# Two transformer blocks on one core: padding the rows of three x buffers in SBUF

## The chip, the cores and the metric

The kernel runs on one core of a Trainium2 chip. The metric is the time of one execution on the device in microseconds (us); lower is better. One execution was also recorded by the profiler, and every row shown here comes from that recording. Engines are called PE (matrix multiply), PEld (its weight load, which overlaps PE), DVE (vector), ACT (scalar), POOL (GpSimd) and SP (which issues most transfers).

## The reference

The input x has 256 rows of 1024 float32 numbers. A first block applies a gated MLP mixer with a spatial 128 x 128 mix, a SwiGLU feed-forward, attention with a relative bias over chunks of 64, a second SwiGLU feed-forward and a norm. A second block runs two layers, each with a mixer (a 31-tap convolution branch, a causal attention branch and a gated linear attention branch, joined and projected) and a feed-forward with a 3-tap convolution, and ends in a norm. Nearly all the arithmetic is in the products `h @ w`, where `h = rms_norm(x, g)` or an activation:

```
h = _rms_norm(x, g_norm);  z = h @ w_in          # gated MLP
gate, up = split(h @ w_gate_up);  y = silu(gate) * up;  x = x + y @ w_down
u = causal_depthwise_conv(h @ ffn_w_up, ...);    x = x + (silu(u0) * u1) @ ffn_w_down
```

## The kernel before

**Weights.** All weights come as a stream of units of 128 partitions x 2048 float32, in four slots (`raw`). For each unit ACT writes a rounded copy `whi` (line 602) and DVE the remainder `wlo` (line 1160), both in the format fp32r. A product of two float32 matrices is then three products in fp32r: high by high, high by low, low by high (`split3`, lines 1875 to 1877). Each matmul has its own weight load.

**x, transposed.** PE turns x (line 1903), DVE multiplies the columns by the norm's gain (`xg`, line 1211), ACT writes the high part `xth` (line 616) and DVE the low part `xtl` (line 1223). Both are tiles of 8 rows (`kt`, one for each 128 of the 1024 model columns) of 256 numbers (the tokens) in every partition. These are the unscaled x: the factor 1/rms of each token is applied later, when a product is read out. An instruction of line 616 or 1223 writes 4 rows, 128 numbers of each.

**Where x is read.** PE reads the tiles in three ways.
- In `in_group` (lines 1875 to 1877) 128 numbers of a row of `xth` or `xtl` are the stationary operand, and 512 columns of `whi` or `wlo` stream past it. The 11th weight part of the mixers does the same with 272 columns of the tiles `whx` and `wlx`, whose rows are 272 numbers (1088 bytes) long and not padded.
- In `kq_step` (lines 2183 to 2186) and in the first feed-forward groups of the second block (`up_straight` for j = 1 and 2, lines 2554 to 2557) the weights are stationary and a whole row of 256 numbers of `xth` or `xtl` streams.
- In `up_straight` for j from 3 to 10 (lines 2545 and 2549) a third tile, `xhl`, streams. Its 8 rows hold the scaled x: 256 high numbers and then 256 low numbers. ACT writes the high halves (line 1086) and DVE the low halves (line 1787), in two instructions each per layer. Line 2545 streams all 512 numbers of a row past `whi`, line 2549 the first 256 past `wlo`.

**Addresses.** Every tile is placed by hand. Offsets such as `o_xh` (of `xth`), `o_xl` (of `xtl`), `o_yh` and `o_yl` (activations), `o_sc` (scratch, `xhl` at `o_sc + 5120`) and `o_c` (constants) are sums of the sizes ahead of them, in float32 numbers from byte 16512 of each partition. The order of work is a fixed list on each engine, held together by semaphores.

Of the kernel before, what the change touches and what calls it, by code (L numbers as in the profile page):

```python
# [21 lines left out]
F32R = mybir.dt.float32r  # L22
# [6 lines left out]
SEQ = 256  # L29
M = SEQ // P  # L30
KT = D // P
# [24 lines left out]
FSEVEN_POS = (6, 8)  # L56


U_IN = 0
U_OUTA = U_IN + 16  # L60
U_GLU0 = U_OUTA + 8
# [23 lines left out]
def two_blocks_kernel(nc, x_in, stream, cols, bs_col, ws_t, gs_row, fin_row, fin2_row, rel_rows, ffn_cw,  # L85
                      conv_w, conv_ln, moba_g, gla_g, gate_w, gate_b, gate_in, out):
    ctx = ExitStack()
    with ctx:
# [5 lines left out]
        def at(name, shape, offset, dt=F32):  # L94
            return nc.alloc_sbuf_tensor_at(name, [P] + shape, dt, offset=base + 4 * offset)
# [2 lines left out]
        o_raw, o_hi, o_lo = 0, SLOTS * UNIT, 2 * SLOTS * UNIT  # L98
        o_x = 3 * SLOTS * UNIT
        o_xh = o_x + M * D  # L100
        o_xl = o_xh + KT * SEQ
        o_yh = o_xl + KT * SEQ
        o_yl = o_yh + 22 * SEQ
        o_sc = o_yl + 22 * SEQ
        o_c = o_sc + 9216
        o_sa, o_sb = o_yh + KT * SEQ, o_yl + KT * SEQ

        raw = at("raw", [SLOTS, UNIT], o_raw)
        whi = at("whi", [SLOTS, UNIT], o_hi, F32R)
        wlo = at("wlo", [SLOTS, UNIT], o_lo, F32R)  # L110
        x = at("x", [M, D], o_x)
        xth = at("xth", [KT, SEQ], o_xh, F32R)
        xtl = at("xtl", [KT, SEQ], o_xl, F32R)
        yth = at("yth", [22 * SEQ], o_yh, F32R)
        ytl = at("ytl", [22 * SEQ], o_yl, F32R)
        yth3 = yth[:, :].rearrange("p (k t) -> p k t", t=SEQ)
# [47 lines left out]
        us = at("us", [2, M, 512], o_sc)  # L164
        cv = at("cv", [2, 4, SEQ], o_sc + 2048)
        pr = at("pr", [2, 2, SEQ], o_sc + 4096)
        xhl = at("xhl", [KT, 2 * SEQ], o_sc + 5120, F32R)

        ysum = at("ysum", [SEVEN * 3 * P], o_sc + 2048)
        ysum_l = at("ysum_l", [SEVEN * 3 * P], o_sc + 2048, F32R)  # L170
# [154 lines left out]
        def pair_bank(pair, m):  # L325
            return acc[(pair % 2) * 2 + m]
# [44 lines left out]
        def wait_group(eng, ct, u, m, t=0):  # L371
            if m == 0:
                eng.wait_ge(m0_done, ct + 1 + 2 * t)
            else:
                eng.wait_ge(unit_used, u + 4 * t)
# [210 lines left out]
        def _(act):  # L586
# [93 lines left out]
            def gmlp_act(j):  # L680
                for m in range(M):
                    wait_group(act, C_IN + j, U_IN + 2 * j + 2, m)
                    if j == 0 and m == 0:
# [1189 lines left out]
        def _(pe):  # L1873
# [5 lines left out]
            def in_group(o, m, U, t=0, a=xth, b=xtl, norm=None, count=0, mid=None, hooks={}):  # L1879

                for half in range(2):
                    s = (U + half) % SLOTS
                    if m == 0:
                        pe.wait_ge(lo_ready, U + half + 1 + 4 * t)
                    if norm is not None:
                        pe.wait_ge(norm, count + 2 * m + half + 1)
                    for kk in range(4):
                        kt = 4 * half + kk  # L1890
                        ts = slice(m * P, (m + 1) * P)
                        ws = slice(512 * kk, 512 * kk + 512)
                        mm = split3(o, a[:, kt, ts], b[:, kt, ts], whi[:, s, ws], wlo[:, s, ws], kt == 0, kt == KT - 1)
                        if kt == 1 and mid is not None:
                            mid()
                        if kt in hooks:
                            hooks[kt]()
                    if m == 1 and half == 0:
                        mm.then_inc(unit_used, 1)
                mm.then_inc(m0_done if m == 0 else unit_used, 1)  # L1900
# [181 lines left out]
            def spatial(m):  # L2082
                if m == 0:
                    pe.wait_ge(a_vn, 2)
                    pe.wait_ge(consts_made, 4)
                for b in range(4):
                    if m == 1:
                        pe.wait_ge(a_spc, b + 1)
                    for g in (2 * b, 2 * b + 1):
                        mm = pe.matmul(tb[b][:, (g % 2) * GDIM:(g % 2 + 1) * GDIM], ws_sb[:, g, :],  # L2090
                                       v_a[:, m, g * GDIM:(g + 1) * GDIM], start=True, stop=True)
                    mm.then_inc(a_sp, 1)
# [12 lines left out]
            for j in range(1, 8):  # L2105
                for m in range(M):
                    if j >= 2:
                        pe.wait_ge(a_ev, 2 * (j - 2) + m + 1)
                    if j == 1 and m == 0:
                        pe.wait_ge(n_gm, 4)  # L2110
                    in_group(pair_bank(j + PAIR_IN, m)[:, :], m, U_IN + 2 * j,
                             hooks={3: (lambda m=m: spatial(m))} if j == 5 else {})
# [556 lines left out]
```

## Time and profile before

| what | value |
|---|---|
| median of 3 runs | 1211.23 us (1210.66 to 1211.8) |
| the profiled execution's own time | 1211.01 us |
| its span, first to last instruction | 1209.3 us |
| PE busy in the span | 1200.8 us |
| DVE busy | 920.8 us |
| ACT busy | 690.6 us |
| granted TensorE clock, mean | 0.999 |

The own time is 1.71 us more than the span, for what lies around the instructions. The median of the three runs is 0.22 us above the profiled execution. The busy time of PE is the union of its matmuls, whose ends are modelled; the distance from one matmul's start to the next one's is the better measure of its rate.

### The profile page before, as it was taken

The numbers are of one execution on the slowest core, as the hardware profiler recorded it, in microseconds if no ns is written. First come the engines' busy times: TensorE is split into PE (matmuls) and PEld (weight loads), VectorE is DVE, ScalarE is ACT, GpSimd is POOL, SyncE is SP. The second block draws the span as 40 slices with busy tenths as digits, with TensorE's granted clock in tenths as the row PEclk, the third lists the DMA queues.
The fourth block names the chain that finished last, engine by engine and source line by source line (L and its number), as shares of the span: only waits on it lengthen the run. The fifth ranks groups of instructions, "written<-read, shape, count | busy, mean of one in ns | idle before, by whom it ended". The sixth has DMA issues, their size and how long they took to land.

```text
span 1209.3 us, 16954 instructions
## 1 busy us (share of the span) xinstructions
PE 1200.8 (99%) x6587; PEld 1020.6 (84%) x6587; DVE 920.8 (76%) x1121; ACT 690.6 (57%) x823; POOL 51.3 (4%) x101
## 2 busy tenths in 40 slices
PE   9999999999999999999999999999999999999998
PEld 7888888888899888888888888988888888988886
DVE  5566465658886685565988995999977998699986
ACT  7655254455465664454548565577644765477752
POOL 2000000000010000000010020000001011000000
PEclk9999999999999999999999999999999999999999
DMA  9644635545654335545464444565564434556550
GB/s 350 234 163 165 229 143 206 184 167 203 241 195 167 132 140 209 196 166 195 174 234 163 151 144 170 174 209 193 191 214 166 150 105 174 181 191 209 186 192 35
DMA packets 32564, 220.34 MB, mean 182 GB/s; under 512 B 3888, under 2 KB 4048, under 8 KB 6768
## 3 DMA queue, kind: packets, MB, share of 16 engines
q1 hardware_dynamic: 29888, 212.33, 49.5%
q0 software_dynamic: 1664, 5.41, 1.3%
q10 hardware_dynamic: 944, 1.64, 0.4%
q8 instruction: 50, 0.82, 0.3%
q14 instruction: 18, 0.15, 0.0%
HBM read 218.31 MB, written 1.05 MB: 181 GB/s over the span
## 4 chain that ended last, share of the span: by engine, by line
PE 92%; DVE 6%; DMA 1%; issue 0%; POOL 0%; ACT 0%; ACTq 0%; POOLq 0%; DVEq 0%
PE acc L1875 21%; PE acc L1877 20%; PE acc L1876 20%; PE acc L2545 5%; PE tb L2545 5%; PE tb L1903 3%; DVE cacc L1551 3%; PE tb L2549 3%; PE acc L2549 3%; DVE wlo L1160 1%; PE acc L2183 1%; PE acc L2185 1%; PE acc L2186 1%; PE tb L1875 1%; PE tb L1877 1%; PE tb L1876 1%
## 5 line engine op out<-in xcount | busy, mean ns | idle before, releaser
L1160 DVE TENSOR_TENSOR wlo<-raw,whi 128x2048 fp32r<-128x2048 f32 x184 | 417.4, 2287 | 120.4 <-ACT whi L602 120.4
L602 ACT ACTIVATE whi<-raw 128x2048 fp32r<-128x2048 f32 (+1 forms) x198 | 368.5, 1882 | 64.6 <-PE acc L1877 52.1
L1875 PE MATMUL acc<-whi,xth 128*128 128x512 f32 x704 | 279.5, 397 | 0.7 <-DVE xtl L1258 0.5
L1877 PE MATMUL acc<-whi,xtl 128*128 128x512 f32 x704 | 274.5, 390 | 0.0
L1876 PE MATMUL acc<-wlo,xth 128*128 128x512 f32 x704 | 274.1, 389 | 0.0
L1875 PE MATMUL acc<-whi,yth 128*128 128x512 f32 (+1 forms) x428 | 168.8, 394 | 0.0
L1877 PE MATMUL acc<-whi,ytl 128*128 128x512 f32 (+1 forms) x428 | 166.5, 389 | 0.0
L1876 PE MATMUL acc<-wlo,yth 128*128 128x512 f32 (+1 forms) x428 | 166.3, 388 | 0.0
L1877 PEld LDWEIGHTS acc<-whi,xtl 128*128 128x128 f32 x704 | 132.1, 188 | 28.2
L1875 PEld LDWEIGHTS acc<-whi,xth 128*128 128x128 f32 x704 | 132.2, 188 | 28.0 <-DVE wlo L1249 1.4
L1876 PEld LDWEIGHTS acc<-wlo,xth 128*128 128x128 f32 x704 | 132.4, 188 | 25.7
L1877 PEld LDWEIGHTS acc<-whi,ytl 128*128 128x128 f32 x428 | 80.3, 188 | 16.9
L1875 PEld LDWEIGHTS acc<-whi,yth 128*128 128x128 f32 x428 | 80.4, 188 | 16.0 <-issue 0.5
L1876 PEld LDWEIGHTS acc<-wlo,yth 128*128 128x128 f32 x428 | 80.4, 188 | 15.7
L740 ACT ACTIVATE sg<-acc,stat 128x256 f32<-128x256 f32 x44 | 20.9, 476 | 93.9 <-PE acc L1877 93.9
L2545 PE MATMUL acc<-xhl,whi 128*128 128x512 f32 x256 | 69.9, 394 | 0.0
L2545 PE MATMUL tb<-xhl,whi 128*128 128x512 f32 x256 | 69.9, 394 | 0.0
L1727 DVE SCALAR_TENSOR_TENSOR cv<-us,fcw,cv 128x255 f32<-128x255 f32 (+1 forms) x160 | 66.7, 479 | 3.3 <-ACT cv L1065 2.6
L1357 DVE SCALAR_TENSOR_TENSOR yy<-acc,stat,sg 128x256 f32<-128x256 f32 x44 | 21.1, 481 | 63.0 <-ACT sg L740 63.0
L1065 ACT ACTIVATE cv<-us,fcw 128x256 f32<-128x256 f32 x80 | 41.6, 591 | 24.0 <-DVE us L1778 24.0
L616 ACT ACTIVATE xth<-xg 128x512 fp32r<-128x512 f32 x28 | 17.7, 633 | 58.7 <-DVE xg L1211 58.7
L1551 DVE SCALAR_TENSOR_TENSOR cacc<-hpad,cw,cacc 128x256 f32<-128x256 f32 x120 | 48.8, 477 | 0.0
(405 smaller groups left out, 1735.4 us busy)
## 6 DMA issues: line engine op xcount, KB each, us to landing
raw<-in_stream SPq DMA_DIRECT2D x200, 1024.0 KB, 4.9
rb<-in_rel_rows POOLq DMA_DIRECT2D x8, 256.0 KB, 3.0
x<-in_x_in ACTq DMA_DIRECT2D x4, 256.0 KB, 7.1
raw<-in_stream SPq DMA_DIRECT2D x2, 512.0 KB, 9.1
gs_sb<-in_gs_row POOLq DMA_DIRECT2D x1, 1024.0 KB, 7.7
frow<-in_fin_row POOLq DMA_DIRECT2D x2, 512.0 KB, 6.0
raw<-in_stream SPq DMA_DIRECT2D x2, 256.0 KB, 6.8
ws_sb<-in_ws_t POOLq DMA_DIRECT2D x1, 512.0 KB, 7.4
```

The lines of the kernel that those rows point to most:

```text
L602: act.activation(whi[:, s, c0:UNIT], raw[:, s, c0:UNIT], ACT.Copy).then_inc(hi_ready, 1)
L1065: o = act.activation(cv[:, j % 2, a, :], up_source(j, pair, a), ACT.Identity, scale=fcw[:, l, c + 2:c + 3], bias=fcw[:, l, c + 3:c + 4])
L1160: dve.tensor_tensor(wlo[:, s, :], raw[:, s, :], whi[:, s, :], ALU.subtract).then_inc(lo_ready, 1)
L1357: dve.scalar_tensor_tensor(yy[:, j % 2, m, :], pair_bank(j + pair, m)[:, 256:512], rms(STATS[k], m), sg[:, j % 2, m, :], ALU.mult, ALU.mul ...
L1551: dve.scalar_tensor_tensor(cacc[:, a, :], src, w, cacc[:, a, :], ALU.mult, ALU.add).then_inc(done, 1)
L1727: o = dve.scalar_tensor_tensor(dst, src, fcw[:, l, c:c + 1], dst, ALU.mult, ALU.add)
L1875: pe.matmul(o, xh, wh, start=first, stop=False)
L1876: pe.matmul(o, xh, wl, start=False, stop=False)
L1877: return pe.matmul(o, xl, wh, start=False, stop=last)
L1903: return pe.transpose(o, i, ident[0:n, 0:n])
L2545: pe.matmul(o, whi[:, s, ws], xhl[:, kt, :], start=kt == 0, stop=False, skip_group_check=True)
L2549: mm = pe.matmul(o[:, 0:SEQ], wlo[:, s, ws], xhl[:, kt, 0:SEQ], start=False, stop=kt == KT - 1, skip_group_check=True)
```

## The change

A row of `xth` and of `xtl` becomes 260 numbers long instead of 256 (1040 bytes instead of 1024), a row of `xhl` 532 instead of 512 (2128 bytes instead of 2048). The added numbers at the end of each row are neither written nor read. Tiles that lie behind move up: `xtl` by 128 bytes, the activations, the scratch area and all that is placed in it by 256 bytes, the constants by 896 bytes. Weight slots and x itself stay. No instruction, wait or transfer is added, removed or reordered.

```diff
+X_PITCH, XHL_PITCH = SEQ + 4, 2 * SEQ + 20
...
-        o_xl = o_xh + KT * SEQ
-        o_yh = o_xl + KT * SEQ
+        o_xl = o_xh + KT * X_PITCH
+        o_yh = o_xl + KT * X_PITCH
...
-        o_c = o_sc + 9216
+        o_c = o_sc + 5120 + KT * XHL_PITCH
...
-        xth = at("xth", [KT, SEQ], o_xh, F32R)
-        xtl = at("xtl", [KT, SEQ], o_xl, F32R)
+        xth = at("xth", [KT, X_PITCH], o_xh, F32R)[:, :, 0:SEQ]
+        xtl = at("xtl", [KT, X_PITCH], o_xl, F32R)[:, :, 0:SEQ]
...
-        xhl = at("xhl", [KT, 2 * SEQ], o_sc + 5120, F32R)
+        xhl = at("xhl", [KT, XHL_PITCH], o_sc + 5120, F32R)[:, :, 0:2 * SEQ]
```

## Rows read from the trace of the kernel before

**Rows 1.** The page: the span, busy times by engine, and PE's granted clock in slices.

```profile
span 1209.3 us, 16954 instructions
PE 1200.8 (99%) x6587; PEld 1020.6 (84%) x6587; DVE 920.8 (76%) x1121; ACT 690.6 (57%) x823; POOL 51.3 (4%) x101
PEclk9999999999999999999999999999999999999999
```

**Rows 2.** Waits of PE: who waited, for whom, us in total, times, longest.

```profile
PE acc L2030 <- POOL idle L453: 1.5, 1, 1.5
PE acc L1903 <- DMA x<-in_x_in: 0.5, 1, 0.5
PE acc L1875 <- DVE xtl L1258: 0.5, 1, 0.5
```

**Rows 3.** Groups by line and form that read x: count | busy, mean ns.

```profile
L1875 PE MATMUL acc<-whi,xth 128*128 128x512 f32 x704 | 279.5, 397 | 0.7 <-DVE xtl L1258 0.5
L2545 PE MATMUL acc<-xhl,whi 128*128 128x512 f32 x256 | 69.9, 394 | 0.0
L2549 PE MATMUL acc<-xhl,wlo 128*128 128x256 f32 x256 | 40.7, 281 | 0.0
L2183 PE MATMUL acc<-xth,whi 128*128 128x256 f32 x64 | 18.4, 287 | 0.0
L2554 PE MATMUL acc<-xth,whi 128*128 128x256 f32 x64 | 18.3, 285 | 0.0
L1875 PE MATMUL acc<-whx,xth 128*128 128x272 f32 x32 | 9.4, 294 | 0.0
```

**Rows 4.** PE timeline, 512 columns past xth and xtl: start us, us, instruction.

```profile
25.04 0.39 PE L1875 MATMUL acc<-whi,xth 128*128 128x512 f32 x1
...
31.16 0.39 PE L1875 MATMUL acc<-whi,xth 128*128 128x512 f32 x1
```

**Rows 5.** PE timeline, rows of xth and xtl streaming, 256 columns.

```profile
752.25 0.28 PE L2554 MATMUL acc<-xth,whi 128*128 128x256 f32 x1
...
756.21 0.28 PE L2554 MATMUL tb<-xth,whi 128*128 128x256 f32 x1
```

**Rows 6.** PE timeline, rows of whx and wlx streaming, 272 columns.

```profile
643.03 0.29 PE L1875 MATMUL acc<-whx,xth 128*128 128x272 f32 x1
...
646.05 0.29 PE L1875 MATMUL acc<-whx,xth 128*128 128x272 f32 x1
```

**Rows 7.** PE timeline, rows of xhl streaming, 4 of 512 and 4 of 256.

```profile
773.34 1.09 PE L2545 MATMUL acc<-xhl,whi 128*128 128x512 f32 x4
774.27 0.63 PE L2549 MATMUL acc<-xhl,wlo 128*128 128x256 f32 x4
...
784.56 1.09 PE L2545 MATMUL tb<-xhl,whi 128*128 128x512 f32 x4
```

**Rows 8.** PE timeline, 512 columns past xth just after a small float32 product.

```profile
652.07 0.40 PE L1876 MATMUL acc<-wlo,xth 128*128 128x512 f32 x1
...
654.38 0.39 PE L1877 MATMUL acc<-whi,xtl 128*128 128x512 f32 x1
```

**Rows 9.** The chain that ended last, one piece of plain float32 matmuls: start, us.

```profile
76.27 3.45 PE tb L2090 x16
```

**Rows 10.** Single lines on ACT and DVE: ns min/median/max, first and last start.

```profile
L616 ACT ACTIVATE xth<-xg x28: 632/632/637, 150.0 to 1022.1; 128x512 fp32r<-128x512 f32 x28
L1078 ACT ACTIVATE yth<-pr x22: 614/618/636, 769.3 to 1159.1; 128x512 fp32r<-128x512 f32 x22
L1223 DVE TENSOR_TENSOR xtl<-xg,xth x28: 679/692/717, 151.1 to 1022.7; 128x512 fp32r<-128x512 f32 x28
L1760 DVE TENSOR_TENSOR ytl<-pr,yth x22: 681/685/693, 770.0 to 1159.8; 128x512 fp32r<-128x512 f32 x22
L1787 DVE TENSOR_TENSOR xhl<-xg,xhl x4: 1218/1219/1221, 762.9 to 1051.4; 128x1024 fp32r<-128x1024 f32 x4
L2545 PE MATMUL acc<-xhl,whi x256: 387/396/398, 767.7 to 1132.9; 128*128 128x512 f32 x128
```

**Rows 11.** Busy time of each engine in the stretch 800 to 900 us.

```profile
800.00:900.00 100.00, 100.00 (x518) 85.41 (x517) 94.06 (x117) 66.63 (x72) 0.00 (x0) 1.00 0.61 208
```

## The prediction

> **What bounds the kernel now.** I read the page first. PE is busy for 1200.8 of 1209.3 us, and its granted clock stands in the top tenth in all forty slices [rows 1], which is the 2.4 GHz level. Then I asked for PE's waits: there are three, 2.5 us together, and each names something of the opening (the first memset, the load of x, the first low part of x) [rows 2]. After that PE never waits for another engine or for a transfer. So the time is the sum of the distances from one matmul's start to the next, some 6,587 of them, plus an opening and an end of a few us. DVE is far from idle: in the densest stretch it works for 94.06 of 100 us while PE shows 100.00 [rows 11]. It keeps up, with 5.94 us to spare in that stretch.
>
> An edit can therefore move the time in two ways only: it changes the distance between matmuls, or it delays another engine so far that PE must wait.
>
> **How many matmuls touch the moved rows.** The groups [rows 3] stand for their like. Lines 1875, 1876 and 1877 with `xth` or `xtl` have 704 each, 2112 together. Line 2545 has 256 with output `acc` and 256 with `tb`, line 2549 the same, 1024 together. Lines 2183, 2185 and 2186 have 64 each, 192. Lines 2554, 2556 and 2557 have 64 for each of two outputs, 384. The 272-column matmuls are three times 32, 96. The sum is 2112 + 1024 + 192 + 384 + 96 = 3808. Of these, 1024 + 192 + 384 = 1600 have an x row as the streaming operand; in the other 2208 x is stationary.
>
> **What a matmul costs now.** I read starts from the timeline, since durations there overlap. With 512 columns, 27 matmuls take 31.16 - 25.04 = 6.12 us, 226.7 ns each, over all eight rows of `xth` and `xtl` and two token halves [rows 4]. With 256 columns, 33 matmuls take 756.21 - 752.25 = 3.96 us, 120.0 ns each [rows 5]. The difference is 106.7 ns for 256 columns, 0.417 ns a column, which is one column per cycle at 2.4 GHz. What is left, 226.7 - 512 x 0.417 = 13.3 ns, is a fixed part of each fp32r matmul. It doesn't change with the row: in both stretches the row number steps every three matmuls and no row stands out.
>
> **Edit 1: rows of `xth` and `xtl` 16 bytes further apart, stationary use.** A weight load reads 128 consecutive numbers inside one row, so the pitch decides only where it starts. The stretch of [rows 4] takes its weights from addresses 1024 and 512 bytes apart, at an even 226.7 ns. The cost I take is 0. But all these starts are multiples of 512 bytes apart from the weight tiles, so no row here shows what a start 16 or 48 bytes off does. The bounds come from the other distances of the same matmul. Just after a small float32 product, 10 matmuls take 654.38 - 652.07 = 2.31 us, 231 ns each [rows 8], 4.3 ns above the settled 226.7. That is the upper bound. The lower bound is that the fixed 13.3 ns goes away.
>
> **Edit 2: the same rows and those of `xhl`, streaming use.** Here there is a row close to the change: `whx` and `wlx` stream with a pitch of 1088 bytes, so that their rows start 64 bytes further along each time. 24 of these take 646.05 - 643.03 = 3.02 us, 125.8 ns each [rows 6]. The settled rule gives 272 x 0.417 + 13.3 = 126.7 ns. So an odd pitch in steps of 64 bytes costs nothing and may save 0.9 ns. For the 1600 streaming matmuls that is between 0 and 1.4 us. I take 0, because 0.01 us resolution on 24 matmuls leaves half of it open and the steps of 16 and 80 bytes are not those of 64.
>
> **`xhl` as it stands.** Eight groups of four 512s and four 256s take 784.56 - 773.34 = 11.22 us, 1402.5 ns a group [rows 7]. Settled distances would give 4 x 226.7 + 4 x 120.0 = 1386.8 ns. The mixed order costs 15.7 ns a group, over 1024 / 8 = 128 groups 2.0 us. This excess can't come from the pitch alone, as the change of length inside a group disturbs the rhythm in the same way as the float32 product does in [rows 8]. I leave it as it is.
>
> **Edit 3: writes of ACT and DVE.** Line 616 writes four pieces at a pitch of 1024 bytes in 632 ns, line 1078 one contiguous piece of the same 512 numbers in 618 ns (medians). Line 1223 takes 692 ns, its contiguous like, line 1760, takes 685 ns [rows 10]. So by the medians pieces cost 14 ns on ACT and 7 ns on DVE, and whatever the new pitch does is bounded by amounts of that size: up or down 14 ns for each of 28 instructions, 0.4 us in all, and the same for the few of `xhl`. It is hidden under PE's queued work, for PE waits for none of them [rows 2]. For `xhl` the cover can be read: the two low halves of the first layer begin at 762.9 us and take 1.22 us each, so they end near 765.3 us, and PE first reads the tile at 767.7 us [rows 10]. 2.4 us of cover stand against some tens of ns. Without cover, the eight norms would each pass on two such instructions, 8 x (14 + 7) ns = 0.2 us.
>
> **Edit 4: tiles behind move by 128, 256 or 896 bytes.** Every operand of the same line at other addresses shows what an address does on ACT and DVE: 614 to 636 ns, 679 to 717 ns, 681 to 693 ns [rows 10]. Suppose each of the 117 DVE instructions between 800 and 900 us took 20 ns more. That is 2.3 us against 5.94 us of idle time [rows 11]. It stays under cover. PE's distances with the activations as stationary operand are those of x, and their starts stay multiples of 128 bytes. No transfer changes in size or number; nothing is queued differently on SP or POOL. Cost 0.
>
> **Sum.** 0 + 0 + 0 + 0 on the profiled execution: span 1209.3 us, own time 1211.0 us. The median shown is 0.2 us above that, so the forecast for the median is 1211.2 us.
>
> **A rule weighed against the trace.** The fixed part in the rows is 13.3 ns per fp32r matmul. The Trainium skill, page "TensorE: Matmul & The Clock Gate", section "Back-to-back issue gap", gives N/2.4 + 2.5 ns for a warm matmul, which is 215.8 ns for 512 columns against 226.7 here. By this rule 10.8 ns of the 13.3 are an extra of this kernel that another layout might remove; on the 3332 matmuls counted in rival C that would be 36 us and a time near 1175 us. The page "SBUF — State Buffer", section "SBUF: two separate sides", says on the other side that PE never waits on anyone at its SBUF ports, and the first page that streaming and weight load have a read port each; by that there is no collision to remove and the sum stays at 0.
>
> **The rivals.** A, slower: the settled rhythm depends on the common alignment of rows and weight tiles. With a start that slips by 16 bytes from row to row, every third matmul of an in-group meets a new offset, and the rhythm never settles. The place is lines 1875 to 1877 with 512 columns, the price 2112 x 4.3 ns = 9.1 us, the time 1220.3 us. For it speaks that distances of 231 ns exist [rows 8]. Against it: they follow a change of kind or length, not of address, and 272-column matmuls with slipping rows are not slower than settled ones [rows 6]. It decides from 1.15 ns a matmul on (2.4 us / 2112).
>
> B, slightly faster: streaming rows that slip gain 0.9 ns as in [rows 6], 1.4 us, and the groups of `xhl` lose their excess of 2.0 us. The time is 1211.2 - 3.4 = 1207.8 us. For it speaks one row; against it that the gain of [rows 6] is at the edge of resolution, and that the excess in [rows 7] goes with the length.
>
> C, much faster: the fixed 13.3 ns is a collision between the streaming read and the next weight load, which start together at equal alignment. The shift by 16 bytes (80 in `xhl`) parts them in seven rows of eight: 3808 x 7/8 = 3332 matmuls x 13.3 ns = 44 us, the time 1167 us. For it speaks that plain float32 matmuls hardly have the fixed part: 16 with 256 columns take 3.45 us, 215.6 ns each, two cycles a column (213.3 ns) and 2.3 ns [rows 9]. Against it: shifts of 64, 128 and 192 bytes between the two reads leave at least 12.4 of the 13.3 ns (125.8 - 113.4) in [rows 6].
>
> That the change doesn't do what it says can't well be: addresses are constants in the instructions.
>
> **How the numbers follow.** No change 0.66, A and lesser forms of it 0.15, B 0.12, C 0.07. The likeliest case gives 1211.2 us, with a range of its own of 1208.8 to 1213.6, which is 0.2% (2.4 us), about what a measurement of this kernel can tell from no change. For 8 in 10, I take in B with two thirds more on the low side (3.4 x 5/3 = 5.7, so 1205.5) and four fifths of A on the high side (1211.2 + 0.8 x 9.1 = 1218.5). Left out are C (0.07) and the upper end of A (about 0.07). Faster is B and C, 0.19; slower is A, 0.15; same is 0.66.
>
> **What would show it.** In the timeline after, [rows 4] and [rows 5] again at 226.7 and 120.0 ns prove edits 1 and 2; a distance that changes with the row number proves an effect of the address. 1402.5 ns a group of `xhl` tells B from no change. Lines 616, 1223 and 1787 within 20 ns of before prove edit 3, and PE's three waits unchanged prove edits 3 and 4. The forecast is wrong if the distances move, in either direction, by more than 0.6 ns a matmul over the 3808, or if a fourth wait of PE appears.

## The result and the profile after

The changed kernel takes 1218.09 us (median of 5 runs, 1218.02 to 1218.41) against 1211.21 us before (5 runs). The ratio is 1.0059 with a 95% interval of 1.0048 to 1.0070. That is 6.9 us slower, near the upper end of the wider range given (1205.5 to 1218.5), above the likeliest case's own range (1208.8 to 1213.6), and not the "no change" that was forecast.

The page after, to be read beside [rows 1]: the span, and the busy times.

```profile
span 1216.5 us, 16954 instructions
PE 1208.8 (99%) x6587; PEld 1019.3 (84%) x6587; DVE 921.1 (76%) x1121; ACT 690.1 (57%) x823; POOL 52.0 (4%) x101
PEclk9999999999999999999999999999999999999999
```

The span is 7.2 us longer. PE's union of matmuls is 8.0 us longer, with the same 6587 matmuls and the same granted clock. DVE and ACT are within 0.5 us of before. PE's waits after (who waited, for whom, us in total, times, longest) stand beside [rows 2]:

```profile
PE acc L2033 <- POOL idle L456: 1.5, 1, 1.5
PE acc L1906 <- DMA x<-in_x_in: 0.2, 1, 0.2
PE acc L1878 <- DVE xtl L1261: 0.2, 1, 0.2
```

They are the same three, and none is longer. This view shows no new wait; one that it does not show comes further down, and it is small (0.6 us). So nearly all of the loss lies in the distances between matmuls while PE has work. (Lines of the changed kernel are three further on than before: 1878 to 1880 are the in-groups.) PE's timeline after, 512 columns past `xth` and `xtl`, answers to [rows 4]:

```profile
27.73 0.39 PE L1878 MATMUL acc<-whi,xth 128*128 128x512 f32 x1
...
34.70 0.39 PE L1878 MATMUL acc<-whi,xth 128*128 128x512 f32 x1
```

30 matmuls take 6.97 us, 232.3 ns each, where it was 226.7. The rows of `xth` and `xtl` streaming past the weights, 256 columns, answer to [rows 5]; those of `whx` and `wlx` to [rows 6]; those of `xhl` to [rows 7]:

```profile
759.50 0.28 PE L2557 MATMUL acc<-xth,whi 128*128 128x256 f32 x1
...
763.39 0.29 PE L2557 MATMUL acc<-xth,whi 128*128 128x256 f32 x1
...
649.41 0.29 PE L1878 MATMUL acc<-whx,xth 128*128 128x272 f32 x1
...
652.43 0.29 PE L1878 MATMUL acc<-whx,xth 128*128 128x272 f32 x1
...
797.74 1.09 PE L2548 MATMUL acc<-xhl,whi 128*128 128x512 f32 x4
...
808.88 1.09 PE L2548 MATMUL tb<-xhl,whi 128*128 128x512 f32 x4
```

33 streaming matmuls take 3.89 us, 117.9 ns each against 120.0: these became faster. 24 of 272 columns take 3.02 us, as before. Eight groups of `xhl` take 11.14 us, 1392.5 ns a group against 1402.5.

Summing the distances from each matmul's start to the next one's over the whole trace, by the operands of the first of the two, gives the ledger:

| matmuls | count | before, us | after, us | difference |
|---|---|---|---|---|
| in-groups, 512 columns past xth and xtl | 2112 | 487.65 | 496.52 | +8.87 |
| rows of xth and xtl streaming, 256 columns | 576 | 69.68 | 68.62 | -1.06 |
| xhl at wlo, 256 columns | 512 | 60.69 | 60.15 | -0.54 |
| xhl at whi, 512 columns | 512 | 118.93 | 118.87 | -0.06 |
| all others | 2874 | | | +0.03 |
| first matmul's start to the last one's | | 1201.93 | 1209.17 | +7.24 |

The in-groups lose 4.2 ns each, and the streams give back 1.7 us. Inside the entries of `xhl` there is a gap that before has not: at the border between two weight parts a group of four took 0.71 us to the next start instead of 0.47. The timeline of all engines shows what PE's next weight load came behind: DVE's remainder `wlo` (the first two lines of the second fence are after, the last two the same border before).

```profile
785.82 0.63 PE L2552 MATMUL acc<-xhl,wlo 128*128 128x256 f32 x4
786.53 1.16 PE L2548 MATMUL tb<-xhl,whi 128*128 128x512 f32 x4
```

```profile
784.10 2.28 DVE L1163 TENSOR_TENSOR wlo<-raw,whi 128x2048 fp32r<-128x2048 f32 x1
786.50 0.76 PEld L2548 LDWEIGHTS tb<-xhl,whi 128*128 128x128 f32 x4 [0.25 <-issue]
...
776.45 2.29 DVE L1160 TENSOR_TENSOR wlo<-raw,whi 128x2048 fp32r<-128x2048 f32 x1
778.85 0.53 PEld L2545 LDWEIGHTS tb<-xhl,whi 128*128 128x128 f32 x3
```

After, the remainder ends at 786.38 us and the load begins at 786.50; before, 778.74 and 778.85. In both the load follows by about 0.12 us, so this border had next to nothing to spare before either. The kernel waits there for `lo_ready`, the semaphore that DVE raises with each remainder, and the profile puts the idle time down to "issue". It happens once in each layer (at 786.2 and 1073.6 us): 0.24 us at the last matmul at `wlo` and 0.08 us at the next one, 0.6 us of the 7.2 in all. The ledger has it inside the two entries of `xhl`. Why DVE comes later against PE at this point in the kernels with slow in-groups is not shown.

ACT and DVE after, single lines, ns min/median/max, answer to [rows 10]; the busy times of the dense stretch 800 to 900 us, in the fence behind, to [rows 11]:

```profile
L619 ACT ACTIVATE xth<-xg x28: 631/632/635, 151.5 to 1029.7; 128x512 fp32r<-128x512 f32 x28
L1226 DVE TENSOR_TENSOR xtl<-xg,xth x28: 679/688/694, 152.7 to 1030.4; 128x512 fp32r<-128x512 f32 x28
L1790 DVE TENSOR_TENSOR xhl<-xg,xhl x4: 1215/1216/1218, 770.6 to 1059.2; 128x1024 fp32r<-128x1024 f32 x4
```

```profile
800.00:900.00 100.00, 100.00 (x529) 85.72 (x529) 95.37 (x126) 68.72 (x75) 0.00 (x0) 1.00 0.60 202
```

The medians move by 0, -4 and -3 ns, and DVE is busy for 95.37 of 100 us, against 94.06 before. The length of the writes has no part in the loss.

### The profile page after: what moved, and what is told of

The parts are those of the page before. It is cut to its first block, busy times and chain, and to the rows that moved or that the text cites. A ratio compares the mean times of both kernels' runs of the same rounds, so it can differ in the third digit from the quotient of the medians.

```text
span 1216.5 us, 16954 instructions
## 1 busy us (share of the span) xinstructions
PE 1208.8 (99%) x6587; PEld 1019.3 (84%) x6587; DVE 921.1 (76%) x1121; ACT 690.1 (57%) x823; POOL 52.0 (4%) x101
## 4 chain that ended last, share of the span: by engine, by line
PE 98%; DMA 1%; DVE 0%; ACTq 0%; issue 0%; ACT 0%; POOLq 0%; POOL 0%
PE acc L1878 22%; PE acc L1879 22%; PE acc L1880 22%; PE tb L2548 5%; PE acc L2548 5%; PE tb L1906 4%; PE acc L2552 2%; PE tb L2552 2%; PE acc L2186 1%; PE acc L2188 1%; PE acc L2189 1%; PE tb L1879 1%; PE tb L1878 1%; PE tb L1880 1%; PE tb L2218 1%; DMA x<-in_x_in 1%
## 5 line engine op out<-in xcount | busy, mean ns | idle before, releaser
L1878 PE MATMUL acc<-whi,xth 128*128 128x512 f32 x704 | 282.4, 401 | 0.2 <-DVE xtl L1261 0.2
L1879 PE MATMUL acc<-wlo,xth 128*128 128x512 f32 x704 | 278.0, 395 | 0.0
L1880 PE MATMUL acc<-whi,xtl 128*128 128x512 f32 x704 | 277.3, 394 | 0.0
```

Of the source, the lines that this page charges most:

```text
L1878: pe.matmul(o, xh, wh, start=first, stop=False)
L1879: pe.matmul(o, xh, wl, start=False, stop=False)
L1880: return pe.matmul(o, xl, wh, start=False, stop=last)
```

## The experiments

All change only where tiles lie. "On" means towards higher addresses, against the kernel before. The recorded expectations call the run with moved bases and no padded row e3. Where a verdict rests on settled distances, I took the 70 stretches of 24 matmuls over `xth` and `xtl` in each trace and the mean of each one's later half.

### Which part of the change does it

Pitch of `xth` and `xtl` alone (the edit is shown against the changed kernel):

```diff
-X_PITCH, XHL_PITCH = SEQ + 4, 2 * SEQ + 20
+X_PITCH, XHL_PITCH = SEQ + 4, 2 * SEQ
```

> Rows of xth and xtl padded by 16 bytes, rows of xhl as before. Theory (the padding of the stationary rows slows the 512-column in-groups): all 2112 in-group matmuls keep the 232.3 ns that the changed kernel shows at their weights wlo (227 before), about +8.9 us, and the 576 streaming matmuls of 256 columns keep their gain of about 1.1 us in sum; time 1219. Rival (the tiles moved behind, or xhl, cost the time): near 1211.

Measured 1219.88 us, ratio 1.0074 (1.0058 to 1.0089). The in-groups lose 9.37 us, the streaming rows of `xth` and `xtl` gain 1.07 us. As expected.

Pitch of `xhl` alone (against the changed kernel):

```diff
-X_PITCH, XHL_PITCH = SEQ + 4, 2 * SEQ + 20
+X_PITCH, XHL_PITCH = SEQ, 2 * SEQ + 20
```

> Rows of xhl padded by 80 bytes alone. Theory: only streaming rows slip, the in-groups stay at 226.7 ns, the 256-column matmuls of xhl go from 118.5 to 117.5 ns (-0.5 us), the 512-column ones stay; time 1210.6, same within the measurement. Rival (xhl carries a part of the loss, for instance by the late operand after the first padded group, where two distances of the changed kernel are 0.3 us too long): 1211.5 or more.

Measured 1209.68 us, ratio 0.9990 (0.9981 to 0.9999). `xhl` at `wlo` goes from 118.5 to 116.5 ns, 1.0 us. This part of the change is a small gain by itself. In the changed kernel the entry shows only 0.54 us of it, because the wait for DVE takes back 0.48 us there.

No pitch at all, but every base address of the changed kernel (against the kernel before):

```diff
-        o_xl = o_xh + KT * SEQ
-        o_yh = o_xl + KT * SEQ
+        o_xl = o_xh + KT * SEQ + 32
+        o_yh = o_xl + KT * SEQ + 32
...
-        o_c = o_sc + 9216
+        o_c = o_sc + 9376
```

> No row padded; xtl, activations, scratch and constants at the very addresses of the changed kernel. Theory: nothing changes, 1211.2, in-groups at 226.7 ns. Rival (the loss comes from the base of xtl or of the activations against the weight tiles): 1214 to 1218.

Measured 1217.52 us, ratio 1.0054 (1.0039 to 1.0070). My theory fell here: without one padded row the kernel is almost as slow as the changed one. The groups by line and form show where (count | busy, mean ns of one):

```profile
L1877 PE MATMUL acc<-whi,xth 128*128 128x512 f32 x704 | 279.6, 397 | 0.7 <-DVE xtl L1260 0.7
L1879 PE MATMUL acc<-whi,xtl 128*128 128x512 f32 x704 | 279.2, 397 | 0.0
L1878 PE MATMUL acc<-wlo,xth 128*128 128x512 f32 x704 | 278.5, 396 | 0.0
```

The first line is as in [rows 3] (279.5 us before). The other two had 390 and 389 ns before. In distances, `wlo,xth` goes from 227.0 to 232.4 ns on average and `whi,xtl` from 230.9 to 236.3, while `whi,xth` stays. While `wlo,xth` streams, the next weight load is that of `xtl`, the one tile that had moved, by 128 bytes. The matmul after it pays too. The activations' products (1308 matmuls) differ by 0.1 us from before, so their move of 256 bytes costs nothing. The 256-column streams of `xth` and `xtl` became faster here too, by 1.2 us over the 576, though no row is padded.

Padded rows of `xth` and `xtl` with the bases kept on multiples of 512 bytes, `xhl` as before (against the changed kernel):

```diff
-X_PITCH, XHL_PITCH = SEQ + 4, 2 * SEQ + 20
+X_PITCH, XHL_PITCH = SEQ + 4, 2 * SEQ
...
-        o_xl = o_xh + KT * X_PITCH
-        o_yh = o_xl + KT * X_PITCH
+        o_xl = o_xh + KT * X_PITCH + 96
+        o_yh = o_xl + KT * X_PITCH + 96
```

> Rows of xth and xtl 1040 bytes apart, but the base of xtl and of all tiles behind on a multiple of 512 bytes from where they were, so that row kt of xth and of xtl lie alike. Theory (the row pitch and the 128 bytes of xtl each do it by themselves): in-groups near 232 ns in the rows that are off, 1217 to 1219. Rival (the whole loss of the change is the 128-byte move of xtl, the padding adds nothing): 226.7 ns and 1210 to 1211.

Measured 1218.9 us, ratio 1.0061 (1.0038 to 1.0084); in-groups +9.04 us. The pitch does it by itself as well. The two causes don't add: 7.6 us of in-groups for the base, 9.0 for the pitch, 8.9 for both.

### Slip or place

Both tiles shifted by a constant, rows 1024 bytes apart as before (this and what follows are shown against the kernel before, unless said otherwise):

```diff
-        o_xl = o_xh + KT * SEQ
-        o_yh = o_xl + KT * SEQ
+        o_xl = o_xh + KT * SEQ + 32
+        o_yh = o_xl + KT * SEQ + 32
...
-        xth = at("xth", [KT, SEQ], o_xh, F32R)
-        xtl = at("xtl", [KT, SEQ], o_xl, F32R)
+        xth = at("xth", [KT * SEQ + 32], o_xh, F32R)[:, 4:4 + KT * SEQ].rearrange("p (k t) -> p k t", t=SEQ)
+        xtl = at("xtl", [KT * SEQ + 32], o_xl, F32R)[:, 4:4 + KT * SEQ].rearrange("p (k t) -> p k t", t=SEQ)
```

> xth and xtl start 16 bytes further on, but their rows are 1024 bytes apart as before. Theory of the offset (a stationary start off the grid of the weight tiles costs time by itself): in-groups at about 232 ns in every row, +8 to +9 us, 1220. Theory of the slip (only a start that changes against the stream from matmul to matmul keeps the rhythm from settling): in-groups settle at one even distance, 226.7 ns, and the time stays 1211.

Measured 1220.36 us, ratio 1.0075 (1.0060 to 1.0091). The kernel was not what I had written of it: the padding put `xtl` 144 bytes on and only `xth` 16. It shows that no slip is needed, but not which offset acts. So the next ones shift both tiles alike (4, 16, 32 and 64 numbers), with the activations and what follows 512 bytes on (shown for 4 numbers):

```diff
-        o_yh = o_xl + KT * SEQ
+        o_yh = o_xl + KT * SEQ + 128
...
-        xth = at("xth", [KT, SEQ], o_xh, F32R)
-        xtl = at("xtl", [KT, SEQ], o_xl, F32R)
+        xth = at("xth", [KT * SEQ + 128], o_xh, F32R)[:, 4:4 + KT * SEQ].rearrange("p (k t) -> p k t", t=SEQ)
+        xtl = at("xtl", [KT * SEQ + 128], o_xl, F32R)[:, 4:4 + KT * SEQ].rearrange("p (k t) -> p k t", t=SEQ)
```

> xth and xtl both start 16 bytes further on, rows 1024 bytes apart, xtl exactly 8192 bytes behind xth as before (in the run before, xtl had come to lie 144 bytes on). Activations and what lies behind move by 512 bytes. Theory of the relation to the stream (a weight load that starts off the place of the stream that passes beside it costs time, whichever way it is off): in-groups at 231 to 235 ns, +8 us or more, 1220. Rival, theory of sameness (only two successive weight loads from unlike places disturb; e3's gap of 128 bytes between xth and xtl did that): in-groups settle at 226.7 ns, 1211.

> The same with 64 bytes. Theory of the relation to the stream with a period of 64 bytes: 226.7 ns and 1211. With a longer period: 231 ns or more, 1219. Theory of sameness: 1211.

> The same with 128 bytes. Theory of the relation to the stream: e3 put xtl alone there and lost 6 us, so both tiles there cost more, in-groups at 231 to 236 ns in all three parts of a product, 1219 to 1223. Theory of sameness: only the unequal places of xth and xtl did it in e3, so 226.7 ns and 1211.

> xth and xtl both 256 bytes on, rows 1024 bytes apart, the rest by 512. 64 and 128 bytes gave 233 ns, multiples of 512 give 226.7. If the place repeats every 256 bytes: settled in-groups at 226.7 ns in all 74 stretches, 1211. If it repeats every 512 or more: about 232 to 233 ns, 1220.

| both on by | time, us | ratio (95%) | in-groups, us | stretches settled at 226.7 ns |
|---|---|---|---|---|
| 16 bytes | 1217.76 | 1.0055 (1.0032 to 1.0077) | +7.0 | 19 of 70, the others at 233.3 |
| 64 bytes | 1222.0 | 1.0089 (1.0059 to 1.0118) | +12.0 | none, all at 233.3 |
| 128 bytes | 1221.14 | 1.0082 (1.0052 to 1.0111) | +9.9 | none, mean 232.7 |
| 256 bytes | 1210.77 | 1.0000 (0.9989 to 1.0010) | +0.5 | 70 of 70 |

PE's timeline of the kernel with 64 bytes:

```profile
28.70 0.39 PE L1877 MATMUL acc<-whi,xth 128*128 128x512 f32 x1
...
35.70 0.39 PE L1877 MATMUL acc<-whi,xth 128*128 128x512 f32 x1
```

and of the kernel with 256 bytes:

```profile
238.08 0.39 PE L1877 MATMUL acc<-whi,xth 128*128 128x512 f32 x1
...
244.88 0.39 PE L1877 MATMUL acc<-whi,xth 128*128 128x512 f32 x1
```

30 matmuls take 7.00 us in the one, 233.3 ns each, and 6.80 us in the other, 226.7 ns. The theory of sameness (only two successive weight loads from unlike places disturb) is dead, since both tiles lie alike in all four. A constant offset does the harm, and 256 bytes do none. The kernel with 16 bytes has two rhythms at the same addresses. Two stretches of it:

```profile
28.16 0.40 PE L1877 MATMUL acc<-whi,xth 128*128 128x512 f32 x1
...
35.16 0.40 PE L1877 MATMUL acc<-whi,xth 128*128 128x512 f32 x1
...
238.56 0.39 PE L1877 MATMUL acc<-whi,xth 128*128 128x512 f32 x1
...
245.36 0.39 PE L1877 MATMUL acc<-whi,xth 128*128 128x512 f32 x1
```

7.00 and 6.80 us for 30. What picks the rhythm is not shown. The addresses modulo 256 are the same in both stretches, so it may be the moment at which a stretch begins.

### Place against what

Weights shifted with x, by 16, 64 and 128 bytes (shown for 64):

```diff
-        whi = at("whi", [SLOTS, UNIT], o_hi, F32R)
+        whi = at("whi", [SLOTS * UNIT + 16], o_hi, F32R)[:, 16:16 + SLOTS * UNIT].rearrange("p (s u) -> p s u", u=UNIT)
```

`wlo`, `xth` and `xtl` get the same shift, x lies 512 bytes on and the activations 1024.

> xth and xtl 16 bytes on as in the run where only they moved (1217.8), and whi and wlo 16 bytes on as well, x itself by 512. Theory of the relation (what counts is where the weight load starts against the stream): the in-groups come back to 226.7 ns in all stretches, and the products of the activations, whose tiles now lie 16 bytes off against whi and wlo, go from 226.7 to between 227 and 233 ns, up to 1284 x 6 = 7.7 us. Rival (the absolute place of the weight load counts): in-groups stay as in the run before, a good half of them at 233 ns, and the activations' products at 226.7.

> whi, wlo, xth and xtl all 64 bytes on; x alone by 512, activations by 1024, so that these lie 64 bytes off against the weights. Theory of the relation with starts on multiples of 64 bytes: in-groups at 226.7 ns, the activations' products near 233 ns (1284 x 6.6 = 8.5 us), in all about 1219. Theory of the absolute place: in-groups stay at 230 to 233 ns as with 16 bytes, 1224 to 1230.

> The same by 128 bytes. Relation: in-groups at 226.7 ns, the activations' products at 231 to 233 ns, 1217 to 1220. Absolute place: in-groups slow too, 1224 to 1230.

| weights and x on by | time, us | ratio (95%) | in-groups | activations' products |
|---|---|---|---|---|
| 16 bytes | 1223.59 | 1.0105 (1.0085 to 1.0125) | no stretch at 226.7 ns, mean 231.3, +8.0 us | +5.4 us |
| 64 bytes | 1211.65 | 1.0006 (0.9996 to 1.0016) | 69 of 70 at 226.7 | +3.0 us |
| 128 bytes | 1218.33 | 1.0061 (1.0041 to 1.0081) | 70 of 70 at 226.7 | +6.8 us |

PE's timeline of the kernel with all four tiles 64 bytes on:

```profile
237.82 0.39 PE L1877 MATMUL acc<-whi,xth 128*128 128x512 f32 x1
...
244.62 0.39 PE L1877 MATMUL acc<-whi,xth 128*128 128x512 f32 x1
```

6.80 us for 30, 226.7 ns, at the very place of x that gave 233.3 ns when the weights stayed behind. So it is the relation of the two tiles that counts. With 128 bytes it is the same, and there the loss turns up in the activations' products, which now are the ones that lie off. With 64 bytes I had expected that loss as well, 8.5 us, and it was 3.0 us: the activations lie 64 bytes short of the weights there, not 64 bytes ahead, and settle near 228.9 ns, not at 233.3. So the direction of an offset counts too. The total of 1211.65 us is close to before only because shorter streams of 256 columns give back what the activations lose: 1.9 us on `xhl` at `wlo` (114.8 ns) and 1.2 us on the activations' own 192. With 16 bytes the relation alone did not bring 226.7 ns back: the stretches settle between 230.0 and 233.3 ns. What the other two runs have besides is a start on a multiple of 64 bytes.

### The streaming rows of xhl

Other steps of the pitch of `xhl`, nothing else padded; 16 numbers more, and in two further kernels 8 and 4 (against the changed kernel):

```diff
-X_PITCH, XHL_PITCH = SEQ + 4, 2 * SEQ + 20
+X_PITCH, XHL_PITCH = SEQ, 2 * SEQ + 16
```

> Rows of xhl 2112 bytes apart instead of 2048, nothing else padded (80 more gave 1209.7). Theory (any slip in the streaming rows frees the 256-column matmuls of some ns): xhl at wlo 116.5 to 117.5 ns, 1209.7 to 1210.5. Rival (it takes steps of 16 bytes): 118.5 ns and 1211.

> Rows of xhl 2080 bytes apart. Theory (any slip): 116.5 to 117.5 ns for the 256-column matmuls of xhl, 1209.7 to 1210.5. Rival (80 bytes are special, or its gain was the phase in which the groups happened to start): 118.5 ns and 1211.

> Rows of xhl 2064 bytes apart. 80 more gave -1.3 us, 32 more and 64 more nothing. If a slip by an odd multiple of 16 bytes does it: xhl at wlo 116.5 to 117 ns, 1209.7. If 80 bytes were a lucky rhythm: 118 to 120 ns and 1211.

Measured 1211.13 us with 64 bytes more, ratio 1.0004 (0.9994 to 1.0013); 1210.80 us with 32, 0.9998 (0.9989 to 1.0008); 1210.06 us with 16, 0.9992 (0.9982 to 1.0002). `xhl` at `wlo` stands at 120.0, 118.1 and 117.8 ns. With 80 bytes it had been 116.5. "Any slip" is refuted. For odd multiples of 16 the times are inconclusive, since the interval of the last touches no change. These averages over all 512 also take in the border at which PE can wait for DVE: with `xhl` where it was, they run from 118.5 to 120.1 ns from kernel to kernel. The 384 distances inside the groups of four are free of it. They are 118.6 ns before and 118.3 to 118.6 ns in every kernel that leaves `xhl` in its old place against the weights, modulo 256 bytes, and 119.7, 117.5 and 117.7 ns with 64, 32 and 16 bytes more; with 80 they are 115.7 ns. So 16 and 32 bytes do gain about 1 ns at each of the 384, 0.4 us, too little for the times to tell.

A constant offset of `xhl`, rows 2048 bytes apart; 48 numbers (192 bytes), and in a second kernel 16 numbers (64 bytes):

```diff
-        xhl = at("xhl", [KT, 2 * SEQ], o_sc + 5120, F32R)
+        xhl = at("xhl", [KT, 2 * SEQ], o_sc + 5120 + 48, F32R)
```

> Only xhl moves, by 192 bytes, which is 64 bytes short of the next place that is alike modulo 256; rows 2048 bytes apart as before; constants 256 bytes on. Theory (the sign and size of the offset decide; 64 bytes behind the weights is good for the streams of 256 columns): xhl at wlo 114.8 ns instead of 118.5, -1.9 us, 1209.1. Rival (the gain came from the phase that the shifted weights brought): 118 to 120 ns, 1211.

> Only xhl moves, by 64 bytes. If the sign counts: no gain or a loss, 118 to 121 ns, 1211 to 1212. If any offset of 64 bytes is good: 114.8 ns and 1209.1.

Measured 1209.29 us with 192 bytes, ratio 0.9985 (0.9976 to 0.9994), and 1208.88 us with 64 bytes, ratio 0.9983 (0.9974 to 0.9993). These are faster than both kernels of this study. The first was foretold to 0.2 us, with 114.8 ns for `xhl` at `wlo`. The second went against my theory of the sign, which had 64 bytes in this direction bring nothing: 115.8 ns there, and 230.7 instead of 232.3 ns at `whi`. Its timeline, beside [rows 7]:

```profile
773.13 1.07 PE L2547 MATMUL acc<-xhl,whi 128*128 128x512 f32 x4
774.04 0.63 PE L2551 MATMUL acc<-xhl,wlo 128*128 128x256 f32 x4
...
775.90 1.07 PE L2547 MATMUL acc<-xhl,whi 128*128 128x512 f32 x4
```

Two groups take 2.77 us, 1385 ns a group against 1402.5.

## Why the prediction was wrong

**What bounds the kernel** was right in the main. 6.6 of the 7.2 us are distances between matmuls that wait for nobody. But "PE never waits for another engine" after the opening left out a border with no cover: PE's load follows DVE's remainder by about 0.12 us there, before and after, and after the change the wait costs 0.3 us in each layer. The busy share of DVE, 5.94 us to spare in 100, could not show that.

**Edit 1, stationary rows: the step that failed.** I took 0 and measured 4.2 ns on each of 2112 matmuls, 8.9 us. The value was read from a stretch whose rows step by 1024 and 512 bytes, "and no row stands out". But both steps are multiples of 256 bytes, so that stretch had only one place in it, and evenness over its rows said nothing of other places. The text saw that no row showed a start 16 bytes off, and still chose 0. The upper bound from [rows 8], 4.3 ns, came out as the measured value by luck: those distances follow another product and fall back to 227 ns after some ten matmuls, and an offset of 64 bytes cost 5.7 ns each (12.0 us / 2112), more than the bound.

**Edit 4, moved bases: wrong too.** I costed the 128 bytes of `xtl` at nothing along with the rest. Alone (with the harmless moves behind it) they cost 6.4 us from first to last matmul. The part of the step on activations held: they moved by 256 bytes and their distances stayed. The reason I gave, that the starts stay multiples of 128 bytes, was no reason: a shift of 128 bytes is harmful. The activations kept their distances because their own move was 256 bytes, and that one is harmless.

**Edit 2, streaming rows: sign as bounded, size beyond it.** I took 0 and allowed a gain of up to 0.9 ns. The 576 matmuls of `xth` and `xtl` gained 1.8 ns each (1.06 us / 576), `xhl` 0.6 us. A slip of the rows is not what it takes: with moved bases and no padded row these 576 gained 1.2 us as well, and with weights and x shifted together by 64 or 128 bytes they gained nothing (0.04 us). The row of `whx` was near in kind, yet its own matmuls didn't move.

**The excess of xhl** I left as it is, holding that it can't come from the address. In part it does: moved by 64 bytes with no pitch, a group takes 1385 ns.

**Edit 3, the writes,** was right on their length: 4 ns at most. Its sign, "PE's three waits unchanged", holds in the view of waits, which does not list the wait for `wlo` told above. Longer writes did not cause that wait: `xtl` and `xhl` took 4 and 3 ns less by the medians.

**Rival A** gave the right sign and place and, by the luck named above, almost the price (9.1 us, measured 8.9), and 1220.3 us, from which the streams' gain takes off 1.7 us. Its mechanism was wrong in one point. I had the start slip from row to row and so keep the rhythm from settling. The runs with a constant offset show that no slip is needed: with 64 bytes the rhythm does settle, only at 233.3 ns. Also "they follow a change of kind or length, not of address", my argument against it, held for [rows 8] and not for what was to come.

**Rival C** has a true grain for the streams: at `wlo`, the 114.8 ns of `xhl` are 106.7 for the columns and 8.1 for the fixed part, against 11.8 before (118.5 - 106.7). For the in-groups the common place is the better one. The Trainium skill, page "TensorE: Matmul & The Clock Gate", section "Back-to-back issue gap", gives N/2.4 + 2.5 ns as the gap of an isolated warm matmul, which would put 256 columns at 109.2 ns; the lowest average of a pair of tiles here was 113.4 (`ytl` at `whi`, 64 matmuls, in the kernel with all four tiles 64 bytes on). What the Trainium skill states on the same page, section "Step-by-step: what each phase is for", of separate read ports for stream and weight load speaks of no relation between their addresses, and the runs show one.

**Sum.** +8.87 - 1.06 - 0.54 - 0.06 = +7.2 us, the difference of the spans; 0.6 us of wait for DVE stand inside the two terms of `xhl`.

**Open.** Why 16 bytes in common do not restore the rhythm, and 64 and 128 do: one run each, and no run with 32. Why the streams of 256 columns prefer another place than those of 512. Why the sign of 64 bytes counts. Why DVE's remainder comes later against PE at that border. What happens inside PE: the runs show that the relation of two addresses sets the distance, not by what mechanism. That "a place repeats every 256 bytes" rests on 256 itself, on the activations' 256, and on the rows of 512 and 1024; other multiples were not tried.

## What to carry to other kernels

A stream of matmuls with one weight load each can depend on where the loaded tile starts against the streamed one. If every tile of a kernel lies on the same place modulo 256 bytes, its trace can't show this, and a "harmless" padding or shift of a base can cost 0.5 to 1%. Before a tile is moved in a kernel that PE bounds, compare the steps in the trace with the step that is planned: evenness over steps of another size is no evidence. After any change of the allocation look at the distance between starts (226.7 or 233.3 ns here), not at busy shares. And where PE's next load always follows another engine's write by the same short time, there is no cover, whatever that engine's share of idle time.

## What the runs showed of the hardware

- With 512 columns of fp32r at the full granted clock and a weight load for each, the distance settles at 226.7 ns when stationary and streamed tile start alike modulo 256 bytes and on a multiple of 64. It settles at 233.3 ns with the stationary tile 64 bytes on, near 228.9 ns with it 64 bytes short (the activations, weights 64 bytes on), and at 226.7 or 233.3 with it 16 bytes on.
- Streams of 256 columns do the opposite: 120.0 ns in common, 117.9 with padded rows. For `xhl` at `wlo` the mean is 118.5 in common, and 114.8 to 115.8 with the stream 64 bytes away on either side.
- At one border of each layer PE's weight load begins about 0.12 us after DVE's remainder ends, before and after. Where PE comes earlier, it waits, and the view of waits names "issue".
- A kernel with no operation changed moved between 1208.9 and 1223.6 us, 1.2%, by the placement of tiles alone.
